# The mean of the last norm: seven of sixteen rows by accumulating DMA instead of VectorE and GpSimd

## What is computed

```
def layer_norm(x, g, b):
    xf = x.astype(jnp.float32)
    mu = xf.mean(-1, keepdims=True)
    var = jnp.square(xf - mu).mean(-1, keepdims=True)
    return ((xf - mu) * lax.rsqrt(var + LN_EPS) * g + b).astype(x.dtype)
...
    f = jnp.einsum('btf,fd->btd', jax.nn.silu(hg) * hu, ffn_w_down)
    x = layer_norm(ALPHA * x + f, ln2_g, ln2_b)
```

## Time and profile before

| | us |
|---|---|
| median of 3 runs | 2052.66 (2051.81 to 2053.83) |
| the profiled execution | 2054.45 |
| its span, from the first to the last instruction | 2052.7 |
| TensorE busy in the span | 1990.8 |
| VectorE, ScalarE, GpSimd busy | 1664.1, 990.5, 396.6 |

### The profile page before, as it was taken

The page is one execution under the profiler, slowest core; times in us unless marked ns, Lnnn a source line. Parts: engine busy times, 40 slices in busy tenths (PEclk is TensorE's granted clock), DMA queues, the critical chain, the costliest instruction groups (busy, mean ns, idle before and its releaser), DMA issues. The chain is left out here.

```text
span 2052.7 us, 42345 instructions
## 1 busy us (share of the span) xinstructions
PE 1990.8 (97%) x15613; PEld 1971.3 (96%) x15613; DVE 1664.1 (81%) x2623; ACT 990.5 (48%) x1503; POOL 396.6 (19%) x552
## 2 busy tenths in 40 slices
PE   8999999999996999999999999999999999999995
PEld 8999999899996999999999999999999999999995
DVE  3698899887699878777777777777777889899898
ACT  4455444433465444454444544444445545454445
POOL 0022223120640211111111111111111121012212
PEclk9999999999998999999999999999999999999998
DMA  6322222123556766667666676776766898779973
GB/s 222 101 76 78 91 78 77 47 83 126 203 155 204 205 177 183 192 178 190 177 184 191 179 190 177 184 191 177 189 172 204 213 244 212 208 192 234 221 176 121
DMA packets 123229, 343.99 MB, mean 168 GB/s; under 512 B 14388, under 2 KB 24884, under 8 KB 123120
## 3 DMA queue, kind: packets, MB, share of 16 engines
q1 hardware_dynamic: 94320, 260.40, 38.0%
q0 software_dynamic: 27792, 80.19, 22.6%
q10 hardware_dynamic: 1008, 1.93, 0.3%
HBM read 314.04 MB, written 23.97 MB: 165 GB/s over the span
## 5 line engine op out<-in xcount | busy, mean ns | idle before, releaser
L1012 PE MATMUL acc<-comb,w_hi 128*128 128x274 f32 x4784 | 922.6, 292 | 21.5 <-DVE comb L2165 12.7
L1012 PEld LDWEIGHTS acc<-comb,w_hi 128*128 128x128 f32 x4784 | 760.7, 190 | 23.3 <-issue 8.5
L1012 PE MATMUL acc<-comb,w_lo 128*128 128x274 f32 x2392 | 693.7, 290 | 0.0
L1012 PEld LDWEIGHTS acc<-comb,w_lo 128*128 128x128 f32 x2392 | 458.7, 192 | 0.0
L1127 PE MATMUL acc<-comb,w_hi 128*128 128x272 f32 x2240 | 424.4, 288 | 3.5 <-DVE w_lo L2303 3.0
L1127 PEld LDWEIGHTS acc<-comb,w_hi 128*128 128x128 f32 x2240 | 352.3, 189 | 5.8 <-DVE w_lo L2303 3.8
L1127 PE MATMUL acc<-comb,w_lo 128*128 128x272 f32 x1120 | 323.4, 289 | 0.0
L1415 ACT ACTIVATE w_hi<-sum 128x1024 fp32r<-128x1024 f32 x172 | 182.3, 1060 | 237.2 <-PE acc L1012 134.5
L2113 DVE TENSOR_TENSOR w_lo<-sum,w_hi 128x1024 fp32r<-128x1024 f32 x172 | 210.8, 1225 | 80.9 <-ACT w_hi L1415 76.4
L2113 DVE TENSOR_TENSOR w_lo<-raw_a,w_hi 128x1024 fp32r<-128x1024 f32 x125 | 152.9, 1223 | 107.5 <-ACT w_hi L1415 107.5
L1127 PEld LDWEIGHTS acc<-comb,w_lo 128*128 128x128 f32 x1120 | 210.8, 188 | 0.0
(11 more groups left out here) (299 smaller groups left out, 3147.3 us busy)
## 6 DMA issues: line engine op xcount, KB each, us to landing
raw_a<-w_up SPq DMA_DIRECT2D x127, 512.0 KB, 6.0
stage<-w_stream SPq DMA_DIRECT2D x90, 512.0 KB, 3.3
sum<-w_up POOLq DMA_DIRECT2D x89, 512.0 KB, 7.1
sum<-w_up SPq DMA_DIRECT2D x88, 512.0 KB, 3.3
d_a<-w_down SPq DMA_DIRECT2D x96, 320.0 KB, 4.6
act_spill<-prod_f SPq DMA_DIRECT2D x43, 272.0 KB, 5.6
d_s<-w_down SPq DMA_DIRECT2D x32, 320.0 KB, 4.5
d_s<-w_down POOLq DMA_DIRECT2D x32, 320.0 KB, 7.2
```

The costliest lines, as they stand in the source:

```text
L1012: mm = pe.matmul(bank(b), wt[:, k * P:(k + 1) * P], prod_comb(j, k, c), start=start and q == 0, stop=stop and q == 2, skip_group_check=True)
```

## The change

Rows 9 to 15 get the mean removed by two DMAs that GpSimd issues as soon as `ln_mu2` is written: one adds it to rows 9, 10 and 11, the other to rows 12 to 15. [...] VectorE keeps the subtractions of rows 0, 1, 4 and 7, GpSimd those of rows 2, 3, 5, 6 and 8. The product of rows 9 to 11 waits for the ninth count of `down_shifted`, that of rows 12 to 15 for the ninth count of `x1_added`.

```
-LATE_SUBS = (0, 1, 4, 7, 10, 13)
+LATE_SUBS = (0, 1, 4, 7)
+DMA_ROWS = ((9, 12), (12, 16))
...
-                act.activation(halves(ln_mus[which][:, toks(which)]), AL(a, which), ACT.Copy).then_inc(stat_used, 1)
+                act.activation(halves(ln_mus[which][:, toks(which)]), AL(a, which), ACT.Copy, scale=-1.0 if which else 1.0).then_inc(stat_used, 1)
...
                 if k in LATE_SUBS:
                     st.wait()
+                elif k >= DMA_ROWS[0][0]:
+                    dve.wait_ge(x1_added if k >= DMA_ROWS[1][0] else down_shifted, 16 * 9)
                 else:
...
-                pool.tensor_tensor(r, r, ln_mus[which][:, toks(which)], ALU.subtract).then_inc(mean_off, 1)
+                pool.tensor_tensor(r, r, ln_mus[which][:, toks(which)], ALU.add if which else ALU.subtract).then_inc(mean_off, 1)
...
             pool.wait_ge(stat_used, 2)
+            pool.wait_ge(down_shifted, 16 * 8)
+            for (a, b), landed in zip(DMA_ROWS, (down_shifted, x1_added)):
+                pool.dma_start(resid[:, a:b, D0:], ln_mu2[:, D0:].unsqueeze(1).broadcast_to([P, b - a, D_TOK]),
+                               accum_op=ALU.add).then_inc(landed, 16)
             for k in range(KT):
-                if k not in LATE_SUBS:
+                if k not in LATE_SUBS and k < DMA_ROWS[0][0]:
                     mean_away(2, k)
```

## The result

The changed kernel takes 2058.51 us in the median of ten runs (2056.07 to 2062.29), against 2052.68 us (2050.19 to 2054.41, ten runs) before: the ratio is 1.0033, with a 95% interval of 1.0024 to 1.0041. It is slower by 5.8 us, 0.28% by the two medians (the ratio on record is 0.33%), and by more than the 0.2% that can be told from no change.

The account below looks back on a forecast made before the run. The DMA engines were taken to bound the tail: first packet at 2035.3, accumulations 10.3 us, stores 11.3 us and 0.85 us to the end gave +5.0 us, a median of 2057.7; the forecast's own range was 2056.2 to 2059.4.

Parts of the forecast that it names:

- The sum: Tail: first packet at 2035.3, accumulations 10.3 us, stores 11.3 us, 0.85 us to the end; span about 2057.7, +5.0 us.
- GpSimd's start: GpSimd ahead of row 2: two DMA issues take 3.6 us, so its additions start at 2037.0 instead of 2033.4.
- The second way: Tail: VectorE waits 2 to 3.5 us before row 12, ScalarE ends 2052.8 to 2054.3, span ends 2056.1 to 2057.6.
- The gain that could have been: Tail: two subtractions fewer save VectorE 1.5 us, but ScalarE is next, so the gain is at most 0.8 us.
- A: Tail: accumulations go at the stores' 384 to 400 GB/s, only GpSimd's late start costs; +1.9 us, median 2054.6; chance 0.17.
- B: Tail: nothing waits, transfers cheap, both issues at most 1.0 us together; 0.8 us less, 2051.9; chance 0.03.
- C: Tail: DMAs worse than their rows (issues 5.9 us, 165 GB/s, or a gap before last stores); median about 2060; chance 0.12.

Follow-up runs that it names:

- the run with the unread accumulations: Changed kernel with its two DMAs adding the same 1.95 MB to memory nobody reads, only the kernel's end waiting for them: 2058.38 us, ratio 1.0032.
- 16 columns: Changed kernel with two accumulating DMAs nobody reads, cut to 16 of 544 columns, rows 9 to 15 keeping their mean: 2053.75 us, ratio 1.0009.
- the run with three rows: Changed kernel with only rows 13 to 15 by one accumulating DMA, VectorE and GpSimd taking the others: 2052.53 us, ratio 1.0002 to before.

## Why the prediction was right

**The bound.** The forecast was +5.0 us and 2057.7; measured were +5.8 and 2058.51. The cause was the one it named: the DMA engines full from the first accumulation to the last store. The run with the unread accumulations shows it, since there the waits for landings are gone and the time stays; the run with copies shows that it is the double engine time of an accumulated byte.

**The sum, term by term**, counted from the end of ScalarE's mean. The first packets were put at 2.0 us and came at 2.7 (2031.93). The two kinds of work were put at 10.3 + 11.3 = 21.6 us without a hole and took 21.9 (2031.93 to 2053.82), and from the last packet to the end it was 0.9 us for 0.85. That makes 25.45 for the forecast's 24.45. Of the 1.0 us short, 0.7 is the start: I had let the issue begin 0.09 us after the mean, as GpSimd's addition did before, and it began 0.83 us after it; from there to the first packet it was 1.84 us, where I had 1.9. The other 0.3 I put down to the accumulations: with the stores at their 11.3 us, 10.6 are left for 1.95 MB, which is 184 GB/s. Alone they moved 0.74 MB in 4 us, 184 GB/s too, close to the earlier trace rows; I had taken 190 as a mean that the faster DMAs from DRAM had pulled up. The shares of the two queues can't confirm this split, since they add up to more than 100%.

**GpSimd's start.** The forecast was 3.6 us for both issues with nothing ahead. The trace has 0.83 us between the end of the mean and the first issue, and 2.61 us for both. The five additions end at 2039.22 and take 1.33 us each in the earlier trace rows, so the first really began about 2032.6, 3.3 us after the mean where I had 3.7. That this came out nearly right is in part luck: the issues were 1.0 us cheaper than the term for them, and the 0.83 us ahead of them were not in the sum. The waits before rows 2 and 3 were 1.68 and 0.57 us where I had 1.9 and 0.65.

**The second way.** I expected the second DMA at 13 us or more after its issue and a wait before row 12 of 2 to 3.5 us: 14.33 and 2.53. The first landed 7.0 us after its issue, before row 9. One step of it was wrong in its detail. I let the first store share the engines at once, from 0.7 us after its issue. SP issued it at 2033.42, and queue 1 has no packet until 2037.5; the view of 2033.5 to 2037.5 holds queue 0 alone:

```profile
q0 software_dynamic: 355, 0.74, 109.6%
```

Since the engines were busy anyhow, this changed nothing in the end. It goes with a sign that I had wrong: queue 0 was to have about 55% of the engines' time until it ends, though 10.3 us in the 13 to 15 us of my own second way are 68 to 78%. In the trace it has 11.3 us of the 12.7 from its first packet to its last data (2044.6), 89%.

**The gain that could have been.** I put it at 0.8 us with ScalarE next; without the DMAs it is 1.0.

**Rivals.** A said that the accumulations are cheap on the engines and that the time would be +1.9. Its condition is wrong here (172 to 184 GB/s and not 384), but its price was nearly right: with the work taken away (16 columns) it is +1.6 in the tail. With copies it is +1.3, but there the engines had no hole and set part of it, so that run doesn't bear out A's price by A's mechanism. The fit of the Trainium skill, page "DMA: Bandwidth & Descriptors", section "Anatomy of one DMA — SWDGE (gpsimd) path", is on A's side, with 2.0 us plus the bytes at 436 GB/s; the first DMA alone would be 3.9 us by this estimate and was 7.0, though no store had a packet before it landed. The copies, at 353 GB/s, are not far from it. B fell with the waits before rows 2 and 3; C was not reached in the median, 2058.51, but two of its ten runs, 2060.59 and 2062.29, lie there; whether it is the tail that was longer in them isn't known, as they have no profile.

## What to carry to other kernels

Work that is moved from an engine to a DMA is not free work: before moving it, add up the engine time of all DMAs in that stretch, count an accumulated byte twice, and see whether the idle time that is there holds it. Here some 4.2 us of the DMA engines' time were idle in the tail; three rows took 4.4 us, and with ScalarE's end 0.6 us later they fitted; seven took about 11 and did not. And where a kernel's early part varies by some microseconds from run to run, compare profiles from a common event on, not by their spans; and test the wait at the head of a chain by removing it before believing that it is what costs. In the changed kernel it wasn't; in the one with GpSimd's rows first the trace has the end hang on it.

## What the runs showed of the hardware

- An accumulating DMA within SBUF moved 172 to 184 GB/s with the engines full (186 to 198 in the slices of the view of 2030 to 2051.5 in the run with three rows), a copy with the same source, issuer and bytes 353, the stores to DRAM 384. The copy used 480 packets, the accumulation 928.
- With both queues at work they get equally many packets: from 2038 to 2044 in the changed kernel queue 0 has 354 and queue 1 has 358, and queue 0 has two thirds of the time, since each of its packets takes twice as long:

```profile
q0 software_dynamic: 354, 0.77, 71.6%
q1 hardware_dynamic: 358, 0.74, 36.9%
```

  The Trainium skill, page "DMA: Bandwidth & Descriptors", section "Queues, rings and completion order", says that an engine goes round its queues packet by packet; the equal counts agree, as far as the profile's packets are the page's, which no run shows. It doesn't account for the first store, which had to wait for 4.1 us before its first packet, against 0.9 in the kernel before. Adding isn't the reason: behind the copies the first store waited too, from 2038.30 to 2041.6, 3.3 us. With three rows it waited for 2.8 us, from 2035.68 to 2038.5, which is when the accumulation's packets gave out. What held it back wasn't tried.
- GpSimd's issue of an accumulating DMA doesn't cost by its bytes: 1.28 us for three rows, 2.61 us for three and four together, with 544 columns as with 16. Copies of the same rows took 1.60 us together. When GpSimd has waited for the mean, its DMA starts 0.83 us after it, an addition 0.09 us after it.
